# The last mixer of a two-block decoder: mask added by TensorE, logits of four heads kept in PSUM, gates spread, tables grouped, final sum by halves

## The reference

```python
def _stick_breaking_attention(q, k, v):      # 8 heads of 64, 256 positions
    for blk in range(2):                     # blocks of 128 queries
        z = einsum("bhqd,bhkd->bhqk", qb, kf[:, :, :kl]) * 64 ** -0.5
        mask = arange(kl)[None, :] < q_pos[:, None]            # strictly causal
        log_one_minus = where(mask, log_sigmoid(-z), 0.0)
        rev = cumsum(log_one_minus, axis=3, reverse=True)
        weights = exp(where(mask, z + rev, -inf))
        outs.append(einsum("bhqk,bhkd->bhqd", weights, vf[:, :, :kl]))

h = rmsnorm(x, norm_b); q, g = split(h @ w_in_b)               # each 512 wide
k, v = split(rmsnorm(x, norm_kv) @ w_kv)
x = x + (o * silu(g)) @ w_out_b                                # 512 -> 1024
return rmsnorm(x, norm_f)
```

## Time and profile before

| | |
|---|---|
| median of 3 runs | 1371.01 us |
| the profiled execution | 1373.02 us |
| its span | 1371.2 us |
| TensorE busy | 1312.3 us (96%) |
| DVE busy | 773.4 us (56%) |
| ACT busy | 675.9 us (49%) |
| GpSimd busy | 132.0 us (10%) |
| mean granted TensorE clock | 0.982 |

### The profile page before, as it was taken

One profiled execution on the slowest core, in us unless ns is written; L12 is line 12 of the kernel. 1 busy time (PEld: TensorE's weight loads), 2 busy tenths in 40 slices (PEclk: granted clock), 3 DMA queues, 4 the chain that ended last, 5 costly groups with the idle time before them and its releaser, 6 DMA issues.

```text
span 1371.2 us, 18373 instructions
## 1 busy us (share of the span) xinstructions
PE 1312.3 (96%) x6964; PEld 1115.4 (81%) x6964; DVE 773.4 (56%) x922; ACT 675.9 (49%) x883; POOL 132.0 (10%) x210
## 2 busy tenths in 40 slices
PE   7999999999789999999999999899999999999977
PEld 5888888998677888888888888688888888997965
DVE  5555545778656555554555545865655544765652
ACT  6544446666445544433544435854554425435541
POOL 3000001028540000000000002600000000000000
PEclk9999999999899999999999999999999999999989
DMA  9655644542134365565555553412655663754301
GB/s 284 206 186 186 218 127 154 184 158 90 62 116 161 121 216 184 184 215 184 172 184 183 188 203 109 153 63 92 196 186 188 226 185 93 203 184 166 124 1 46
DMA packets 179758, 218.78 MB, mean 160 GB/s; under 512 B 8585, under 2 KB 132814, under 8 KB 179694
## 3 DMA queue, kind: packets, MB, share of 16 engines
q1 hardware_dynamic: 178318, 216.70, 48.3%
q10 hardware_dynamic: 1088, 1.05, 0.2%
q0 software_dynamic: 288, 0.15, 0.1%
HBM read 216.82 MB, written 1.05 MB: 159 GB/s over the span
## 4 chain that ended last, share of the span: by engine, by line
PE 86%; DVE 8%; ACT 4%; issue 2%; DMA 0%; POOL 0%; POOLq 0%; ACTq 0%; SPq 0%; DVEq 0%
PE acc L570 26%; PE acc L572 25%; PE acc L571 25%; PE tr L587 3%; DVE w_lo L1731 2%; ACT w_hi L1193 1%; PE tr L817 1%; PE aux L959 1%; DVE conv L1946 1%; ACT xT_hi L1206 1%; PE acc L940 1%; DVE E L1904 0%; DVE xT_lo L1756 0%; PE aux L1085 0%; PE aux L1086 0%
## 5 line engine op out<-in xcount | busy, mean ns | idle before, releaser
L1731 DVE TENSOR_TENSOR w_lo<-raw,w_hi 128x2048 fp32r<-128x2048 f32 (+1 forms) x196 | 440.9, 2277 | 191.1 <-ACT w_hi L1193 191.0
L1193 ACT ACTIVATE w_hi<-raw 128x2048 fp32r<-128x2048 f32 (+1 forms) x198 | 368.9, 1900 | 118.5 <-PE acc L572 118.4
L570 PE MATMUL acc<-w_hi,xT_hi 128*128 128x512 f32 (+1 forms) x914 | 363.1, 397 | 7.3 <-DVE w_lo L2289 4.2
L572 PE MATMUL acc<-w_hi,xT_lo 128*128 128x512 f32 (+1 forms) x914 | 356.4, 390 | 0.0
L571 PE MATMUL acc<-w_lo,xT_hi 128*128 128x512 f32 (+1 forms) x914 | 356.0, 390 | 0.0
L570 PEld LDWEIGHTS acc<-w_hi,xT_hi 128*128 128x128 f32 x914 | 173.0, 189 | 43.2 <-issue 4.7
L572 PEld LDWEIGHTS acc<-w_hi,xT_lo 128*128 128x128 f32 x914 | 172.7, 189 | 36.5
L571 PEld LDWEIGHTS acc<-w_lo,xT_hi 128*128 128x128 f32 x914 | 173.3, 190 | 33.6
L570 PE MATMUL acc<-w_hi,hT_hi 128*128 128x512 f32 x448 | 176.7, 394 | 3.5 <-DVE hT_lo L1756 2.6
L571 PE MATMUL acc<-w_lo,hT_hi 128*128 128x512 f32 x448 | 175.1, 391 | 0.0
L572 PE MATMUL acc<-w_hi,hT_lo 128*128 128x512 f32 x448 | 175.1, 391 | 0.0
(11 more groups left out here) (282 smaller groups left out, 1172.3 us busy)
## 6 DMA issues: line engine op xcount, KB each, us to landing
raw<-in_ffn_w_down SPq DMA_DIRECT2D x88, 512.0 KB, 4.8
raw<-in_ffn_w_gate SPq DMA_DIRECT2D x87, 512.0 KB, 4.4
raw<-in_ffn_w_up SPq DMA_DIRECT2D x87, 512.0 KB, 5.5
raw<-in_ssm_w_in SPq DMA_DIRECT2D x48, 512.0 KB, 4.6
raw<-in_w_in_a SPq DMA_DIRECT2D x64, 256.0 KB, 4.1
raw<-in_ssm_w_out SPq DMA_DIRECT2D x16, 512.0 KB, 4.3
raw<-in_mla_w_out SPq DMA_DIRECT2D x8, 512.0 KB, 4.5
raw<-in_w_out_a SPq DMA_DIRECT2D x8, 512.0 KB, 4.4
```

What stands on the lines that cost most here:

```text
L570: pe.matmul(o, lh, rh, start=start, stop=False, skip_group_check=skip)
L572: return pe.matmul(o, ll, rh, start=False, stop=stop, skip_group_check=skip)
L1193: inst = act.activation(w_hi[:, u % RING, 0:n], raw[:, u % RING, 0:n], ACT.Copy)
L1731: inst = dve.tensor_tensor(w_lo[:, u % RING, 0:n], raw[:, u % RING, 0:n], w_hi[:, u % RING, 0:n].bitcast(F32), ALU.subtract)
```

## The change

All of it is in the last layer and the final norm.

- **Mask.** `scores` adds the mask of 0/-1e30 to the logits at once, by one bf16 matmul of 256 columns (two strided blocks of 128) with `ident_b`. DVE then reads masked logits, and a masked place gives a softplus of 0; the product with `zmask`, and GpSimd's making of it, are gone. `from_` and `ones` hold -1 in place of 1.
- **Logits kept.** Heads 0 to 3 have their logits in `tr` and `aux` and keep them there: `weights(hd)` for them is only `from_` over all 384 columns and `ones` over 128. Heads 4 to 7 have their first logits in two free `acc` banks and are computed again in `weights`. The weights use all four banks of `tr` and `aux`, `wt` has three buffers, and TensorE's order is weights 0 to 3, then values(hd), weights(hd + 4).
- **Gates spread.** The gates are done tile by tile: two tiles of the first half-unit, logits 0 to 5, one tile, logits 6 and 7, the last tile, then the four tiles of the second half-unit.
- **DVE's order.** Logits 0 to 5, the split of one output unit, logits 6 and 7, four additions of two heads each, the split of the other output unit.
- **ACT's order.** Rounding of both output units, Exp of heads 0 to 3, Exp of heads 4 to 7, Ln in four pieces of two heads, Silu of the gates, Exp for the weights. `xT_hi` of a pair of heads is done after the weights of the next pair; `og` has two buffers.
- **Final sum.** tb = 1 is summed by halves: all of the first 512 columns, then all of the other 512. DVE adds each half when it is done, ACT squares each by itself, GpSimd adds the two sums, DVE scales and SP stores by halves (256 KB each).
- ACT makes one more bf16 copy (`strict_b`) during the first feed-forward layer, and `strict` moves into a region that is reused.

```diff
+WTS = 3
@@ TensorE @@
+            def feature_tile(u, p, k0, ft, done=False):
+                pe.wait_ge(lo_ready, u + 1)
+                for kk in range(4):
+                    k = k0 + kk
+                    w = slice(kk * 512 + ft * P, kk * 512 + ft * P + P)
+                    last = product(bank(p, ft // 2)[:, ft % 2 * T:(ft % 2 + 1) * T], w_hi[:, u % RING, w], w_lo[:, u % RING, w],
+                                   xT_hi[:, k, :], xT_lo[:, k, :], k == 0 and ft % 2 == 0, k == KD - 1, skip=True)
+                if done:
+                    last.then_inc(unit_used, 1)
...
-                    part(n, tb)
+                    if c.next != "end" or tb == 0:
+                        part(n, tb)
+                if c.next == "end":
+                    for nh in range(2):
+                        claim(p + 1, nh)
+                        for k in range(k_tiles):
...
+                        last.then_inc(last_half, 1)
...
                     pe.matmul(o[:, 0:T], ks[:, 0:P], qs, start=True, stop=False, skip_group_check=True)
-                    pe.matmul(o[:, 0:T], from_[:], zl0, start=False, stop=False, skip_group_check=True)
-                    pe.matmul(o[:, P:T], ones[:], zl1, start=False, stop=False, skip_group_check=True)
-                    pe.matmul(o[:, 0:P], ident[:], strict[:], start=False, stop=True, skip_group_check=True)
-                    o1 = o[:, T:3 * P]
-                    pe.matmul(o1, ks[:, P:T], qs[:, P:T], start=False, stop=False, skip_group_check=True)
-                    pe.matmul(o1, from_[:], zl1, start=False, stop=False, skip_group_check=True)
-                    return pe.matmul(o1, ident[:], strict[:], start=False, stop=True, skip_group_check=True)
+                    pe.matmul(o[:, T:3 * P], ks[:, P:T], qs[:, P:T], start=False, stop=False, skip_group_check=True)
+                    return pe.matmul(heads(o, 2)[:, :, 0:P], ident_b[:], strict_b[:].unsqueeze(1).to_broadcast([P, 2, P]),
+                                     start=False, stop=True, skip_group_check=True)
...
+                    if hd < 2:
+                        claim_turn(k0 + hd)
+                    elif hd >= 6:
+                        pe.wait_ge(z_read, hd - 1)
+                    scores(hd, first_bank(p0, hd)).then_inc(z_ready, 1)
...
+                gates(0, 0)
+                gates(0, 1)
+                for hd in range(6):
+                    logits(hd)
+                gates(0, 2)
+                logits(6)
+                logits(7)
+                gates(0, 3)
+                for ft in range(4):
+                    gates(1, ft)
...
                 def weights(hd):
+                    pe.wait_ge(zl_ready, hd // 2 + 1)
+                    o = z_bank(hd)
+                    if hd >= 4:
+                        pe.wait_ge(w_ready, hd - 3)
+                        scores(hd, o)
+                    zl = zr[hd // 4][:, hd % 4, :]
+                    pe.matmul(o[:, 0:3 * P], from_[:], zl, start=False, stop=False, skip_group_check=True)
+                    pe.matmul(o[:, P:T], ones[:], zl[:, T:], start=False, stop=True, skip_group_check=True)\
+                        .then_inc(w_sum, 1)
...
-                weights(0)
-                weights(1)
+                for hd in range(4):
+                    weights(hd)
                 for hd in range(SH):
                     values(hd)
-                    if hd + 2 < SH:
-                        weights(hd + 2)
+                    if hd + 4 < SH:
+                        weights(hd + 4)
@@ ACT @@
+                for four in range(2):
+                    act.wait_ge(z_read, 4 * four + 4)
+                    exped = act.activation(zn[four][:], zn[four][:], ACT.Exp)
+                link(exped)
+                for four in range(2):
+                    for two in range(2):
+                        at = zn[four][:, 2 * two:2 * two + 2, :]
+                        act.activation(at, at, ACT.Ln, bias=1.0).then_inc(z_ln, 1)
+                act.wait_ge(unit_used, c.unit)
+                for b in range(2):
+                    acc_free(act.activation(s_g[:, 2 * b:2 * b + 2, :].rearrange("p f t -> p (f t)"),
+                                            bank(c.pair, b), ACT.Silu), c.pair, b)
...
+                for b in range(2):
+                    acc_done(act, c.pair - 1, b)
+                    at = slice(512 * b, 512 * b + 512)
+                    act.activation(junk[:, at], x[:, 1, at], ACT.Square, accum_out=square_sum[:, TB + b:TB + b + 1])\
+                        .then_inc(squared, 1)
@@ DVE @@
+                for hd in range(6):
+                    logits(hd)
+                split_to(c.unit + 3)
+                logits(6)
+                logits(7)
+                for two in range(SH // 2):
+                    soft(two)
+                split_to(c.unit + 4)
@@ SP @@
-                sp.dma_start(out[0, b * P:(b + 1) * P, :], xn[:, b, :]).then_inc(stored, 16)
+                for nh in range(2):
+                    at = slice(512 * nh, 512 * nh + 512)
+                    sp.wait_ge(result_ready, 2 * b + nh + 1)
+                    sp.dma_start(out[0, b * P:(b + 1) * P, at], xn[:, b, at]).then_inc(stored, 16)
```

More of the change, by code:

```diff
@@ L421, in z_bank, with first_bank @@
             return (tr if hd % 4 < 2 else aux)[:, hd % 2, :]
+        def first_bank(p0, hd):
+            return z_bank(hd) if hd < 4 else bank(p0, hd % 2)
         def matrix(w):
@@ L1109, in stick @@
+                    scores(hd, first_bank(p0, hd)).then_inc(z_ready, 1)
+                for b in range(TB):
+                    claim(c.pair, b)
+                first_step(lambda half, tb: token_unit(c.unit + half, c.pair, 4 * half, 4, KD, 512,
+                                                       tbs=(tb,), done=tb == 1))
+                c.unit += 2
+                c.pair += 1
+                for n in range(2):
                     for b in range(TB):
                         claim(c.pair, b)
-                    if n == 0:
-                        first_step(lambda half, tb: token_unit(c.unit + half, c.pair, 4 * half, 4, KD, 512,
-                                                               tbs=(tb,), done=tb == 1))
@@ L1114, in stick, with gates @@
                     for half in range(2):
[L1115 to L1119, removed]
+                        feature_unit(c.unit + half, c.pair, 4 * half)
                     c.unit += 2
                     c.pair += 1
+                def gates(half, ft):
+                    feature_tile(c.unit + half, c.pair, 4 * half, ft, ft == 3)
@@ L1123, in stick @@
+                for b in range(TB):
+                    claim(c.pair, b)
+                gates(0, 0)
[8 more added lines that the diff above has]
+                    gates(1, ft)
+                c.unit += 2
+                c.pair += 1
                 c.turn += 4
-                p0 = c.pair
@@ L1643, in stick @@
                 layer_input()
-                def soft(four):
-                    act.wait_ge(z_read, 2 * four + 2)
-                    for r in (1, 2):
-                        turn_done(act, c.turn + 2 * four + 2 - r)
-                    link(act.activation(zn[four][:], zn[four][:], ACT.Exp))
-                    act.activation(zn[four][:], zn[four][:], ACT.Ln, bias=1.0).then_inc(z_ln, 1)
-                for n in range(4):
+                for n in range(3):
                     split_to(c.unit + 4)
@@ L1803, in sums @@
                         dve.wait_ge(landed_x, 16)
-                for tb in range(TB):
+                if c.next == "end":
+                    last_sums(scale)
+                for tb in range(TB if c.next != "end" else 0):
                     if tb:
@@ L2245, in stick @@
[L2245 to L2259 removed]
+                    dve.wait_ge(unit_used, c.unit)
@@ new lines, in stick, with logits @@
+                    dst = (s_v[:, 1, :], s_kT[:, 2:4, :].rearrange("p f t -> p (f t)"),
+                           s_qT[:, 2:4, :].rearrange("p f t -> p (f t)"))[n]
+                    acc_free(dve.tensor_scalar(dst, bank(c.pair, 1), 0.125 if n == 2 else 1.0, None, ALU.mult),
+                             c.pair, 1)
+                    c.pair += 1
+                p0 = c.pair + 1
+                def logits(hd):
+                    dve.wait_ge(z_ready, hd + 1)
+                    z, above = first_bank(p0, hd)[:, 0:3 * P], zr[hd // 4][:, hd % 4, :]
+                    link(dve.tensor_scalar(above, z, 0.0, None, ALU.max))
+                    dve.scalar_tensor_tensor(zn[hd // 4][:, hd % 4, :], above, -2.0, z, ALU.mult, ALU.add)\
+                        .then_inc(z_read, 1)
@@ new lines, in stick @@
+                logits(7)
+                for two in range(SH // 2):
+                    soft(two)
+                split_to(c.unit + 4)
+                c.unit += 2
+                c.pair += 1
+                for j in range(SH // 2):
+                    p, b = c.pair + j // 2, j % 2
+                    dve.wait_ge(heads_done, 2 * j + 2)
```

(8 more changed lines are left out.)

184 lines of the change are left out of this document (72 added, 112 removed).

## The result

The changed kernel took 1351.08 us, the median of 4 runs (1350.61 to 1353.82), beside 1370.34 us for the kernel before (4 runs, 1366.93 to 1373.47). The ratio is 0.9864, with a 95% interval of 0.9837 to 0.9892: 1.4% faster, 19.3 us by the medians. The forecast was 1353.3 us, 17.7 less than before. Both kernels were run again later on another occasion: 1353.45 (6 runs) beside 1369.64 (the 15 of 17 runs of the kernel before that were not in the chip's slower state), 16.2 us by the medians. The ratio there is 0.9839 (0.9783 to 0.9895), further from 1 than the medians' 0.988, as three of those 15 runs took 1385 to 1387 us.

The account below looks back on a forecast made before the run. TensorE, busy 96% of the span, was taken as the bound; 16.5 us from an earlier output product and 1.2 from the tail made 17.7 us, for 1353.3 us against the median, range 1349.5 to 1359.5.

Parts of the forecast that it names:

- The chain and TensorE's order: Last layer, from q's copy-out: first value at 24.7 us, output product at 38.7 us.
- the last four values: End of the heads on TensorE: 0.8 and three times 0.65 without weights between, 2.8 us.
- Idle time and spreading: Last layer: TensorE's idle 7.48 us covered by gates; less the 0.8 us left, 6.7 us.
- ACT's chain as the next bound: Before the values: ACT's Silu table, Silus, Exp table and first Exp set their start, TensorE waiting 0.8 us.
- Logits of 1.05 a head: TensorE's logits with mask and row changes: 1.05 us a head, eight heads 5.2 us more than before.
- The clock's 4.5 us: First two weights: half clock made them 5.0 us each and not 2.76; removing it saves 4.5 us.
- Its 16.5 us: Output product starts at 1335.8 and not at 1352.27, 16.5 us earlier.
- Short of the 3.7 us after which it fell: Pause before the values: 0.8 us, too short for the clock to fall, so the 4.5 us stays won.
- The rival in which the clock falls and stays down: Values' wait reaches 3.7 us, half clock lasts until the output product is through: 1381 us; chance 2%.
- The table rival: ACT's path: each table load also empties the engine, three add 3.8 us, half clock costs 5: 1362 us; chance 4%.
- The tail: After the last matmul: DVE add, ACT square and last store by halves save 1.2 us (bounds 0.8 and 1.8).
- The low end of the range: All low ends (logits 0.76, a round 0.35 shorter, tail 1.8) save 20.3 us: 1350.7 us.

Follow-up runs that it names:

- the first experiment: Changed kernel with logits placed as before, four heads behind each half-unit of gates: median 1362.98 us, ratio 0.9924 to the kernel before; layer 64.5 us.
- Pairs: Changed kernel with heads in pairs, both logits then both masks, rounds of two heads: median 1352.09 us, ratio 0.9832 to the kernel before; layer 52.7 us.
- one pause filled: Kernel before with 31 matmuls in the 7.5 us in which TensorE waited: median 1377.41 us, ratio 1.0026; layer 82.1 us.
- longer pause: Changed kernel with two more ACT table changes between Silus and first Exp of the weights: median 1358.29 us, ratio 0.9896 to the kernel before; layer 61.7 us.
- the last version: Changed kernel with pairs, earlier logits, Exp and Ln by fours, later Silus and splits: median 1347.38 us, ratio 0.9797 to the kernel before; layer 48.3 us.

## Why the prediction was right, and where it wasn't

- **The chain and TensorE's order** (first value 24.7, product 38.7): right to 0.1 and 0.6 us. Of the 0.6, 0.5 is the last four values, 2.3 us where 2.8 was forecast: two of them ran side by side, which the sum has one after the other. The experiments move the chain as the argument said: without the spreading +8.9, with the logits computed twice +2.8, with two table changes more +3.0.
- **Idle time and spreading.** The gates cover DVE's reading and ACT's Exp and Ln. Shown by the first experiment, with the 2.2 us of the split's place in it.
- **ACT's chain as the next bound.** Shown: it sets the first value, and cutting it by 1.5 us brought 1.4. I had it as a 0.8 us pause; it was 1.41, since a weight of heads 0 to 3 costs 0.87 (384 and 128 columns without the 0.1 that I put for starting).
- **Logits of 1.05 a head.** Measured 1.06. The price of the changes between 64 and 128 rows was read from the earlier trace rows. Pairs cost 0.59 a head; of the 0.47 between, 0.33 is the lost running side by side (half of the 0.65 of columns) and the rest the second pair of changes, an estimate from these rows. The Trainium skill, TensorEngine Tiling (Array Packing), Key Properties, says that a change of tiling mode drains TensorE. The trace agrees: a head with its two changes costs 0.3 us more than its columns (0.65) and its mask (0.11).
- **The clock's 4.5 us is not what the clock alone is worth.** Half clock made the first two weights longer by that much, but 1.5 us of it lay under ACT's chain: 3.0 by the run with one pause filled. The forecast did not rest on it. Its 16.5 us is the difference of two positions of the output product, and the list of terms only divides that up, so this mis-sized share left the sum as it was.
- **"Short of the 3.7 us after which it fell" was no argument.** The clock fell after pauses of 1.53 and 1.98 us, and not after 1.41 in three profiles of kernels with the changed order. That the changed kernel kept it was forecast, but for a reason that does not hold: with a pause of 1.41 us beside 1.53, this part of the forecast was luck. The rival in which the clock falls and stays down did happen, in the kernel before with its pause filled: 24 us at half clock.
- **The table rival** (a drain beside each load) is refuted: 1.28 us for each added change.
- **The tail**: 1.4 and not 1.2 us. Scaling in halves takes 1.42 us where the whole took 1.28, which I had left out, and the last store of 256 KB needed 2.4 us from the end of DVE's work (1346.8) where 512 KB needed 3.0; I had taken off only 0.15.
- **The low end of the range** doesn't come out of its parts: 17.7 with the rounds' 1.4 and the tail's 0.6 is 19.7 us and not 20.3. Shorter logits would not have added to it, since DVE reads them at 1.05 us each.
- **The remaining 3.6 us of the profiled spans** lie ahead of the layer, where nothing but one small copy changed. In the kernel before two windows read

```profile
200.00:300.00 100.00, 96.25 (x756) 93.01 (x755) 67.43 (x110) 60.53 (x81) 4.77 (x6) 0.97 0.51 169
...
1100.00:1200.00 100.00, 97.40 (x605) 87.54 (x605) 55.17 (x65) 43.51 (x54) 1.48 (x4) 0.98 0.58 164
```

and after the change 0.98 and 1.00, 3 us of lost clock less between them. The changed kernel's second profile had q's copy-out 2.7 us later than its first, so most of this can be scatter. Whether any part of it belongs to the change (a region of memory moved by some 250 bytes) was not tested by itself; it stays open.

## What to carry to other kernels

Write the chain from the producer to the first consumer as positions on each engine, not as a list of savings: the terms overlapped (the clock's by 1.5 us, the kept logits' by 1.4), the positions were right to 0.1 us for the first value and 0.6 for the output product. Table loads are free where the engine waits anyway; before grouping them, look at which side of the wait the grouped work lands. And pauses of TensorE of 1.5 us ahead of short matmuls can cost more than themselves, so removing a pause can be worth more, and make the runs steadier, than its length says.

## What the runs showed of the hardware that I had not expected

- The clock fell after pauses of 1.53 us (one pause filled), 1.98 (pairs), 4.42 (longer pause), 7.84 (logits by halves) and 7.48 (before), and not after 1.16 (pairs, the last version) or 1.41 us. Once the matmuls resumed it came back after 25, 4.5, 6.2, 4.1 and 9.9 us in that order.
- An even and an odd head on the two halves of the rows: 1.18 us for both with their masks, 2.12 one after the other. Values of two heads in a row on the two halves of the columns also overlap: 0.81 us for both, about what one head takes alone (0.80).
- A DVE scaling of 512 elements took 0.75 us, more than half of the 1.285 for 1024.
